# ScalarE as a third requester of cache pages, and the first keys of two sample stages asked for one stage ahead

## The reference

```python
past = tuple(gather_pages(c, li, page_table) for c in (cache_sb_k, cache_sb_v, cache_dsa_k, cache_dsa_v, cache_idx_k))
...
z = einsum('bqhd,blhd->bhql', q, k) * D_HEAD ** -0.5          # stick-breaking, 8 heads
after = cumsum(log_keep, axis=3, reverse=True) - log_keep
w = where(mask, exp(log_beta + after), 0.0);  o = einsum('bhql,blhd->bqhd', w, v)
...
score = einsum('bqh,bqhl->bql', w_idx, relu(einsum('bqhd,bld->bqhl', q_idx, k_idx)))   # index scores, 8 heads
_, sel = top_k(where(causal, score, -inf), 256)
p = softmax(logits over sel);  o = p @ v                       # sparse attention, 8 query heads, 2 kv heads
```

## Time and profile before

| | us |
|---|---|
| median of 3 runs | 5399.53 (5394.25 to 5403.45) |
| profiled execution | 5401.57 |
| its span | 5399.8 |
| index stage of the samples | 1010.9 to 1107.3 |
| stick-breaking of the samples | 1107.3 to 1507.1 |
| sparse attention of the samples | 1507.1 to 1689.0 |
| from request to landing, median, SP's index pages | 1.8 |

### The profile page before, as it was taken

One profiled execution on the slowest core, in us unless ns is written; L12 is line 12 of the kernel. 1 busy time (PEld: TensorE's weight loads), 2 busy tenths in 40 slices (PEclk: granted clock), 3 DMA queues, 4 the chain that ended last, 5 costly groups with the idle time before them and its releaser, 6 DMA issues. The chain is left out here.

```text
span 5399.8 us, 75557 instructions
## 1 busy us (share of the span) xinstructions
PE 4599.8 (85%) x30371; PEld 2899.1 (54%) x30371; DVE 2292.2 (42%) x3248; ACT 1088.0 (20%) x1971; POOL 350.0 (6%) x523
## 2 busy tenths in 40 slices
PE   8997777777767799999996999577777879999997
PEld 5663223344434466665663645376765546666564
DVE  1248997369921323232004122487685242323102
ACT  1004333344431122221000010222122022222000
POOL 0000000410063000000000000111110000000000
PEclk9998987889978899999997989788888889999998
DMA  2110000289964011111101221412213201111111
GB/s 92 47 39 27 1 0 1 52 288 352 357 181 139 24 35 39 35 39 47 33 22 58 71 82 61 164 30 53 57 30 142 63 24 39 35 39 46 35 33 43
DMA packets 434190, 398.60 MB, mean 74 GB/s; under 512 B 71613, under 2 KB 351717, under 8 KB 429494
## 3 DMA queue, kind: packets, MB, share of 16 engines
q1 hardware_dynamic: 419042, 347.23, 20.2%
q0 software_dynamic: 12288, 21.00, 1.4%
q10 hardware_dynamic: 2584, 26.50, 1.3%
HBM read 341.43 MB, written 53.06 MB: 73 GB/s over the span
## 5 line engine op out<-in xcount | busy, mean ns | idle before, releaser
L2086 PE MATMUL fup_acc<-h,w_up_first 128*128 128x352 f32 x2112 | 636.8, 462 | 28.1 <-ACTq L2093 28.1
L2086 PE MATMUL fup_acc<-h,fup_w 128*128 128x352 f32 x2112 | 632.0, 459 | 0.0
L2086 PEld LDWEIGHTS fup_acc<-h,w_up_first 128*128 128x128 f32 x2112 | 403.5, 191 | 255.4 <-ACTq L2093 30.2
L2086 PEld LDWEIGHTS fup_acc<-h,fup_w 128*128 128x128 f32 x2112 | 401.3, 190 | 223.5
L2129 DVE TENSOR_SCALAR fup_c<-fup_u,taps 128x1072 f32<-128x1072 f32 x88 | 73.7, 838 | 852.1 <-ACT last_u L2106 852.1
L310 PE MATMUL proj_acc<-hT,w_in 128*128 128x352 f32 (+1 forms) x1152 | 344.0, 462 | 1.8 <-DVEq L318 1.8
L1970 PE MATMUL fdown_acc<-hidden,w_down_first 128*128 128x352 f32 x1056 | 317.4, 463 | 0.0
L1970 PE MATMUL fdown_acc<-hidden,fdown_w 128*128 128x352 f32 x1056 | 314.5, 460 | 2.4 <-DVE h L1889 2.4
L310 PEld LDWEIGHTS proj_acc<-hT,w_in 128*128 128x128 f32 (+1 forms) x1152 | 215.4, 187 | 129.9 <-issue 12.4
L1970 PEld LDWEIGHTS fdown_acc<-hidden,w_down_first 128*128 128x128 f32 x1056 | 202.1, 192 | 115.7 <-issue 6.5
L2099 ACT ACTIVATE fup_u<-fup_acc 128x704 f32<-128x704 f32 x88 | 66.7, 757 | 974.6 <-PE fup_acc L2086 974.6
(11 more groups left out here) (582 smaller groups left out, 6846.5 us busy)
## 6 DMA issues: line engine op xcount, KB each, us to landing
sstick_own<-in_cache_sb_k SPq DMA_DIRECT2D x128, 256.0 KB, 5.8
qb<-in_cache_sb_k SPq DMA_DIRECT2D x128, 256.0 KB, 6.2
qi<-in_cache_sb_v SPq DMA_DIRECT2D x128, 256.0 KB, 5.8
ka<-in_cache_sb_v SPq DMA_DIRECT2D x128, 256.0 KB, 6.2
w_up_first<-in_ffn_w_up SPq DMA_DIRECT2D x44, 512.0 KB, 3.7
fup_w<-in_ffn_w_up SPq DMA_DIRECT2D x44, 512.0 KB, 3.8
w_down_first<-in_ffn_w_down SPq DMA_DIRECT2D x8, 1408.0 KB, 7.0
fdown_w<-in_ffn_w_down SPq DMA_DIRECT2D x8, 1408.0 KB, 7.0
```

The source lines that it names most:

```text
L2086: last = pe.matmul(acc[u][:, c, 0:CW], w[u][:, k, :], hT[:, k, c * CW:(c + 1) * CW], start=(k == 0), stop=(k == KD - 1))
```

## The change

Four things change.

1. In the index stage ScalarE becomes a third requester. It asks for unit 3 of every group; SP takes units 0 and 1 of even groups and unit 0 of odd ones, POOL unit 2 of even groups and units 1 and 2 of odd ones. `load` takes a count. ScalarE asks for groups 0 and 1 before its loop and for group g + 2 behind `copy_keys(g)`, ahead of `relus(g - 1)`.
2. SP loads the step order of the page table into `K.pages_steps` (the memory of two constant tiles that only the prompt's stages read) in the index stage, behind its loads of group 2, and at its list's end asks for the first 16 key pages of stick-breaking (`ask_step_keys`). The tile `own_keys` now lives over the three stages. The stick-breaking stage no longer loads the table and begins SP's list with the value loads.
3. At the end of SP's list in the stick-breaking stage SP asks for the first 8 units (32 pages) of sparse keys (`ask_unit_keys`), into `A.qa`.
4. In the sparse stage SP and POOL leave out the keys of groups 0 and 1 and the values of groups 0 to 3. ScalarE asks for those values: in each of the first eight groups two units (eight pages), between `copy_keys(g)` and `take(g - 1)`.

```diff
@@ -879,7 +879,40 @@
     return values
 
 
-def stage_stick_sample(nc, K, A, I, O, oT):
+def half_columns(t, i):
+
+    return t[:, i // 2, i % 2 * 512:i % 2 * 512 + 512]
+
+
+STEP_PAGES = 16
+UNITS_AHEAD = 8
+
+
+def step_key_slot(A, own, i):
+
+    return own[:, i, :] if i < STEP_PAGES // 2 else half_columns(A.qb, i - STEP_PAGES // 2)
+
+
+def ask_step_keys(nc, eng, K, A, I, own, arrived):
+
+    kc = I.cache_sb_k[0].rearrange("n p h d -> n p (h d)")
+    for t0 in range(0, STEP_PAGES, 8):
+        numbers = page_numbers(nc, eng, K.pages_steps[0], 4 * NPG - 8 - t0, 8, kc.shape[0])
+        for i, number in enumerate(numbers):
+            eng.dma_start(step_key_slot(A, own, t0 + i), kc[bass.ds(number, 1)].rearrange("o p n -> p (o n)")).then_inc(arrived[t0 + i], 16)
+
+
+def ask_unit_keys(nc, eng, K, A, I, arrived):
+
+    kc = I.cache_dsa_k[0].rearrange("n p g d -> n p (g d)")
+    for n in range(UNITS_AHEAD):
+        numbers = page_numbers(nc, eng, K.pages_units, n * 4, 4, kc.shape[0])
+        slot = half_columns(A.qa, n).rearrange("p (u n) -> p u n", u=4)
+        for u, number in enumerate(numbers):
+            eng.dma_start(slot[:, u, :], kc[bass.ds(number, 1)].rearrange("o p n -> p (o n)")).then_inc(arrived[n], 16)
+
+
+def stage_stick_sample(nc, K, A, I, O, oT, own):
 
     CP = 2
     CK = CP * PAGE
@@ -897,8 +930,6 @@
     paged = [j for j, st in enumerate(steps) if st[1] is not None]
     n_pages = NB * NPG
     with Stage(nc, "sstick") as s:
-        pages = s.sb("pages", [1, n_pages], I32)
-        own = s.sb("own", [P, KR // 2, 512])
 
...
@@ -922,12 +953,13 @@
         z = [s.ps(f"z{i}", [P, 512]) for i in range(2)]
         wtp = s.ps("wtp", [P, 512])
         o = [s.ps(f"o{i}", [P, 512]) for i in range(2)]
...
-        k_in = [s.sem(f"k_in{i}") for i in range(KR)]
+        k_in, next_in = K.step_keys_in, K.unit_keys_in
+        s.sems += k_in
         v_in = [s.sem(f"v_in{i}") for i in range(VR)]
         block = s.block()
 
@@ -936,19 +968,13 @@
 
         @block.sync
         def _(sp):
-            with nc.allow_non_contiguous_dma(reason="1 KiB of page numbers, in the order of the loads"):
-                for b in range(NB):
-                    half, b4 = b // 4, b % 4
-                    dst = pages[0:1, half * 4 * NPG:(half + 1) * 4 * NPG].rearrange("o (m b) -> o m b", b=4)[:, :, b4]
-                    sp.dma_start(dst, I.page_table[b:b + 1, :]).then_inc(table, 16)
             for half in range(2):
                 sp.dma_start(vnew[:, half, :], O.sb_v_s[0][half * 4:half * 4 + 4].rearrange("b t h d -> (b t) (h d)")).then_inc(new_v, 16)
-            sp.wait_ge(table, 16 * NB)
             k_numbers, v_numbers = {}, {}
 
             def numbers(p):
                 half, c, _ = steps[paged[p]]
-                return page_numbers(nc, sp, pages, half * 4 * NPG + c * PP, PP, n_pool)
+                return page_numbers(nc, sp, K.pages_steps[half], c * PP, PP, n_pool)
 
             def load_k(t):
                 if t % PP == 0:
@@ -966,12 +992,11 @@
                 number = v_numbers[t // PP][t % PP]
                 sp.dma_start(vring(t % VR), vc[bass.ds(number, 1)].rearrange("o p n -> p (o n)")).then_inc(v_in[t % VR], 16)
 
-            for t in range(KR):
-                load_k(t)
             for t in range(n_pages):
                 if t + KR < n_pages:
                     load_k(t + KR)
                 load_v(t)
+            ask_unit_keys(nc, sp, K, A, I, next_in)
 
         @block.gpsimd
         def _(pool):
@@ -1201,7 +1226,7 @@
             dve.wait_ge(o_taken, 16)
 
 
-def stage_index_sample(nc, K, A, I):
+def stage_index_sample(nc, K, A, I, own):
 
     L = PAST + NQ
     G = 4
@@ -1228,13 +1253,13 @@
         (built, laid, small, small_taken, steps, turned, copied, product, relued, chunk_done, chunk_taken) = (
             s.sem(x) for x in ("built", "laid", "small", "small_taken", "steps", "turned", "copied", "product",
                                "relued", "chunk_done", "chunk_taken"))
-        arrived = [s.sem(f"arrived{i}") for i in range(NR)]
+        arrived, tabled = [s.sem(f"arrived{i}") for i in range(NR)], s.sem("tabled")
         block = s.block()
         N = len(groups)
 
-        def load(eng, g, first):
-            numbers = page_numbers(nc, eng, K.pages_units, g * 16 + first * G, 2 * G, n_pool)
-            for j in range(2):
+        def load(eng, g, first, count):
+            numbers = page_numbers(nc, eng, K.pages_units, g * 16 + first * G, count * G, n_pool)
+            for j in range(count):
                 n = g * 4 + first + j
                 if n >= NR:
                     eng.wait_ge(turned, (n - NR) // 2 + 1)
@@ -1246,7 +1271,14 @@
         @block.sync
         def _(sp):
             for g in range(N):
-                load(sp, g, 0)
+                load(sp, g, 0, 2 - g % 2)
+                if g == 2:
+                    with nc.allow_non_contiguous_dma(reason="1 KiB of page numbers, in the order of the loads"):
+                        for b in range(NB):
+                            dst = K.pages_steps[b // 4].rearrange("o (m b) -> o m b", b=4)[:, :, b % 4]
+                            sp.dma_start(dst, I.page_table[b:b + 1, :]).then_inc(tabled, 16)
+            sp.wait_ge(tabled, 16 * NB)
+            ask_step_keys(nc, sp, K, A, I, own, K.step_keys_in)
 
         @block.gpsimd
         def _(pool):
@@ -1258,7 +1290,7 @@
                 pool.affine_select(out=t[:], in_=t[:], compare_op=ALU.is_equal, fill=0.0, base=0, pattern=pattern,
                                    channel_multiplier=mul).then_inc(built, 1)
             for g in range(N):
-                load(pool, g, 2)
+                load(pool, g, 2 - g % 2, 1 + g % 2)
 
         @block.tensor
         def _(pe):
@@ -1351,8 +1383,12 @@
                     act.wait_ge(chunk_done, g - 1)
                 act.activation(relu[:, g % 2, :].rearrange("p (r n) -> p r n", r=2), prod[g % 2][:, :, 0:HK], ACT.Relu).then_inc(relued, 1)
 
+            load(act, 0, 3, 1)
+            load(act, 1, 3, 1)
             for g in range(N):
                 copy_keys(g)
+                if g + 2 < N:
+                    load(act, g + 2, 3, 1)
                 if g >= 1:
                     relus(g - 1)
             relus(N - 1)
@@ -1410,7 +1446,7 @@
     N = len(groups)
     with Stage(nc, "ssparse") as s:
         logit = [s.sb(f"logit{i}", [P, L]) for i in range(2)]
-        turned_w = s.sb("turned_w", [P, 2, CH])
+        turned_w = K.own_keys[:, 0:2, :]
         kT = s.sb("kT", [P, 2, 4, CH])
         bias = A.score[0:NS, 0:L]
         qd = s.sb("qd", [P, NB, 2, HP, NQ])
@@ -1427,7 +1463,8 @@
          o_scaled, o_turned, o_taken, new_v) = (s.sem(x) for x in (
              "built", "laid", "steps", "turned", "copied", "biased", "x_prod", "x_taken", "topped", "maxed", "exped",
              "p_turned", "p_taken", "valued", "o_ready", "o_scaled", "o_turned", "o_taken", "new_v"))
-        k_in = [s.sem(f"k_in{i}") for i in range(KR)]
+        k_in, v_early = [s.sem(f"k_in{i}") for i in range(KR)], [s.sem(f"v_early{i}") for i in range(VR)]
+        s.sems += K.unit_keys_in
         v_in = [s.sem(f"v_in{i}") for i in range(VR)]
         block = s.block()
 
@@ -1451,11 +1488,12 @@
                        .then_inc(arrived[n % size], 16)
 
         def load_all(eng, first):
-            for c in range(NC):
+            for c in range(UNITS_AHEAD // 4, NC):
                 load(eng, c, first, kc, kring, KR, turned, k_in)
             for c in range(NC):
                 load(eng, NC + c, first, kc, kring, KR, turned, k_in)
-                load(eng, c, first, vc, vring, VR, valued, v_in)
+                if c >= VR // 4:
+                    load(eng, c, first, vc, vring, VR, valued, v_in)
             for c in range(NC):
                 load(eng, NC + c, first, vc, vring, VR, valued, v_in)
 
@@ -1482,7 +1520,10 @@
             def turn(g):
                 for b4 in range(4):
                     n = g * 4 + b4
-                    pe.wait_ge(k_in[n % KR], 16 * G * (n // KR + 1))
+                    if n < UNITS_AHEAD:
+                        pe.wait_ge(K.unit_keys_in[n], 16 * G)
+                    else:
+                        pe.wait_ge(k_in[n % KR], 16 * G * ((n - UNITS_AHEAD) // KR + 1))
                     if n >= 3:
                         pe.wait_ge(copied, n - 2)
                     for u in range(G):
@@ -1542,7 +1583,10 @@
                             continue
                         v = (half * NC + c) * 4 + b4
                         if u == 0:
-                            pe.wait_ge(v_in[v % VR], 16 * G * (v // VR + 1))
+                            if v < VR:
+                                pe.wait_ge(v_early[v], 16 * G)
+                            else:
+                                pe.wait_ge(v_in[v % VR], 16 * G * (v // VR))
                         last = pe.matmul(dst, turned_w[:, n % 2, at:at + NS], vring(v % VR)[:, u, :], start=(c == 0 and u == 0), stop=False,
```

(9 more changed lines are left out.)

4 lines of the change are left out of this document (2 added, 2 removed).

## The result

The changed kernel takes 5360.86 us (median of 4 runs, 5357.48 to 5364.35) beside 5400.68 us before (4 runs): ratio 0.9928, 95% interval 0.9911 to 0.9945, or 39.8 us less. The forecast was 5370, 30 us less. The profiled execution took 5363.65 us; its span is 5361.8 us, the mean granted clock 0.916. One of the ten executions of the kernel with extra requests on POOL (further down) took 6450.75 us at a mean clock of 0.704 and is left out of its ratio.

The account below looks back on a forecast made before the run. POOL's issue time for page requests was taken to bound the index and sparse stages, VectorE being full in stick-breaking. Terms -10 - 3 - 17 = -30 us gave 5370 us; own range 5358 to 5382, widened to 5345 to 5394.

Parts of the forecast that it names:

- the index term: Index stage: sharing page requests with ScalarE shortens it by 10 us, bounds -17 and -3.
- the sparse term: Sparse stage: fewer POOL batches against a longer ScalarE cycle of 7.8 us, -17 us, bounds -28 and -5.
- The rival of DMA engines as the bound: Sample stages: only moved bytes count, 14 us won, 5386 us in all; chance 0.05.
- 4.1 per group: no longer the bound: Index stage: POOL's requests and reads take 8.2 us per pair of groups, so POOL stops setting the pace.
- ScalarE's 4.41: Index stage, us per group on ScalarE: copies and ReLU 1.80, read of numbers 0.53, four requests 2.08.
- TensorE's 5.25: Index stage: us per group on TensorE at its lower clock level, taken for half of the groups.
- The table's lag: Index stage: SP's eight table loads, 5.04 us, make its group 3 just in time; 0.5 us allowed.
- Stick-breaking, -3 forecast: Stick-breaking: 5.3 us less waiting at the start, 2.2 us more at SP's end; bounds -6 and 0.
- Better overlap: Requests run ahead of ScalarE's copies, TensorE holds full clock: index -17, stick -5, sparse -28, 5350 us; chance 0.22.
- TensorE bound at the lower level: TensorE's lower clock level sets the pace: index -3, stick -1, sparse -6, 5390 us; chance 0.16.
- Slower, dear request: ScalarE page requests cost 1.0 us, index break-even 0.80: index +12, sparse +11, stick -3, 5420 us; chance 0.07.
- the rule that was weighed: Descriptor generator locked per request: ScalarE's would cost about 0.66 us behind SP's, the sum near -18.

Follow-up runs that it names:

- the index part alone: Kernel before with only ScalarE added as third requester of index pages, no table load and no early keys: 5379.12 us beside 5401.16, ratio 0.9962.
- the three-way values: Changed kernel with ScalarE also asking for unit 3 of sparse value groups 4 to 15: 5351.08 us, ratio to before 0.9899.
- the run with late step keys: Changed kernel, but the first 16 stick-breaking key pages are asked for at the start of their own stage: ratio to before 0.9939.
- the mean of seven: Mean sparse stage of seven kernels (the changed one and six variants) with the same code in that stage: 166.1 us, from 162.2 to 169.1.
- e12: All edits of e11, and in the index stage ScalarE asks for unit 2 of every fourth group in POOL's place: 5348.42 us, ratio to before 0.9913.
- e11: Changed kernel with table loaded ahead, late step keys, POOL asking for first sparse keys, and later sparse values split three ways: 5345.07 us, 0.9882.

## Why the prediction was right, and where a size was off

**Direction and the sum.** POOL's issue time was the bound of both stages, and taking requests off it made them shorter: shown by the index part alone, by the extra requests on POOL, and by the three-way values. That the total came within the forecast's own range of 5358 to 5382 is partly luck: the index term was 10 us short and outside its own bounds (-17 to -3), and the sparse term 3 us too large. The rival of DMA engines as the bound is out: 0.59 busy in the index stage after, and 0.86 in the busiest part of the sparse stage, where places in the rings were waited for.

**Index, -10 forecast, -20.4 measured.** The step that mis-sized this term is "4.1 per group: no longer the bound", and with it the mean of ScalarE's 4.41 and TensorE's 5.25. POOL's 4.1 (3.99, since a read of four numbers costs it 0.42 and not 0.66) was the longest. Had the sum gone by it, 15 x (5.53 - 4.1) = 21.5. ScalarE's 4.41 added up what partly overlaps: the read is hidden, the first request can start beside a copy, and a group with four requests takes as little as 2.59 us. The price of the requests themselves was about right: 1.8 to 1.9 us in 12 of the 16 groups (2.08 forecast), 2.25 to 2.80 in the other four, where one request alone took 0.70 to 1.28 us. Groups of 5.2 us do occur, as at 1065.39 to 1070.62, but they are made up for by groups of 2.59, and a pair takes 7.8, about POOL's 8.0. A mean over clock levels was the wrong way to join two limits; the slowest list with a ring behind it sets the average. The table's lag, put at 0.5, was 1.8, and through all the middle of the stage TensorE waited for SP's pages because of it.

**Stick-breaking, -3 forecast, -4.9 measured.** VectorE's idle time at the start is 5.1 us shorter (5.3 forecast) and the overhang cost 2.0 (2.2 forecast), which is the -3; the rest of the -4.9 is what VectorE's chain varies by. What was wrong is the reason: TensorE's 4.36 us wait for the first page was the table load's doing, and the keys asked for a stage ahead bought nothing, which the run with late step keys shows.

**Sparse, -17 forecast, -14.1 in the profile, -15.7 by the mean of seven.** This term had its mechanism right, ScalarE's longer cycle in the first half and POOL's list in the rest. The cycle was put at 7.8 us and is 7.26 ((1542.42 - 1498.89) / 6 between logit copies), with the eight requests in 3.8 to 5.2 us. First transposition of the second half 63.0 us after POOL's first request (65.7 forecast), value group 4 at 77.6 (77.1), POOL's rest 82.3 (78.5): of these 3.8 us one wait is 1.84, the others are batches cut in two, 0.25 to 0.43 each. The trace of before had 81.8 for the same batches, so the 78.5 could have been read there. The lower bound, -28, is not its own sum either: with a cycle of 6.8 POOL would end at 93.2 + 54.4 = 147.6, -26.4. The part up to value group 4 varies by 7 us in the seven runs of the same code, and with it the granted clock: from the first transposition of the second half to value group 4 it takes 11.8 us at 1.00, 13.1 at 0.89, 14.6 to 15.5 at 0.67 to 0.74 and 16.6 at 0.62. So TensorE's level counts in that stretch.

**The rivals.** "Better overlap" came nearest in the index stage (-17 there), but not by its mechanism: most of ScalarE's request time lies behind its copies, not beside them, and the clock was 0.80, not full. Its -28 in the sparse stage did not come. "TensorE bound at the lower level" and "Slower, dear request" are out: four requests of ScalarE beside SP's and POOL's took 1.83 to 1.94 us in 12 groups of 16 and 2.80 at most, 0.46 to 0.70 each, below the 0.80 of break-even. The trace also speaks on the rule that was weighed. If every ScalarE request first waited out SP's whole 0.33 it would take some 0.66. Of the 64 in the index stage 39 began while one of SP's was running, and lasted 0.35 us in the median, as the other 25 did (0.36); four lasted 0.70 to 1.28, each ending together with a long one of SP's. The Trainium skill, Perfetto Trace Analysis, section DMA Instruction - HWDGE, has the descriptor generator locked for exclusive use while a request is made. These rows show no wait for another's whole request at this load, outside the four long ones. The Trainium skill, DMA: Bandwidth & Descriptors, section Issuing engines are not separate DMA queues, says that further requesters save only sequencer time. That is what was saved, and here it was 20 of 96 us.

**The signs named ahead.** The index stage near 86 us and ScalarE's copies 4.8 apart: no, 76.0 and 4.05. POOL ending well before the last group: no, 3.5 us before its copies. Transpositions right behind the first product, and SP's requests ending behind VectorE's last copy: yes. First half of the sparse stage 62 us: 61.6, from 1484.02 to 1545.61, by TensorE's transpositions: yes.

**What stays open.** Why the clock is granted differently in the sparse stage in runs of the same code; what makes a single request of SP or ScalarE last 0.6 to 1.4 us now and then, where 0.33 is usual (SP has four such in the index stage before, too); whether SP's list or ScalarE's bursts hold e12's index stage; and whether e11 and e12 differ at all in the whole time.

## What to carry to other kernels

When pages are asked for one by one, sum each requester's list (requests and reads of numbers) for the stage: the longest list is the pace as long as a ring lies behind it, and a compute engine's slow groups are made up for. Then look whose pages are waited for: a few small loads put SP's list back by 5 us, and it was waited for over most of the stage. Requests on a compute engine hold up the work behind them in its list; four at a time fell into time in which it would have waited anyway, eight at a time made TensorE wait. So price them by adding dummy requests before giving them away. Moving a request one stage ahead helps only if something waited for it; look at what else that wait was behind.

## What the runs showed of the hardware

- The time to read page numbers into registers goes with their count: four 0.30 to 0.32 us, eight 0.52 to 0.56, on SP, ScalarE and POOL alike (POOL loses 0.42 and 0.66 between requests).
- A request of 16 bytes costs nearly what one of a page does: 0.51 beside 0.577 us on POOL, and on ScalarE 0.83 us for two beside 1.83 to 1.94 for four. The page requests also take their number out of a register, so a part of the difference is that.
- ScalarE issued requests while its own ACTIVATE ran (starts at 1586.18 and 1586.19 us), but an ACTIVATE that stood behind requests started only when they were out (3.97 us idle before 1512.92). Of the request time 5.1 of 32.6 us lay beside an ACTIVATE in the index stage of the changed kernel, and none of 33.3 us in its sparse stage.
- One request of ScalarE and one of SP now and then last 0.7 to 1.3 us together, ending within 0.01 us of each other (1069.38 to 1070.51 on ScalarE, 1069.43 to 1070.51 on SP).
- The second part of the sparse stage on POOL took 82.3 us in each of seven runs, and its last index request was out after 65.6 us in every run with that list: a full request list is the steadiest thing in these traces.
